# A layer step of a hybrid decoder on one NeuronCore: selected-value pages with two tokens in a row, and one copy of the turned probabilities

## The chip, the cores and the metric

The kernel runs on one core of one Trainium2 chip. The metric is device time in microseconds of one execution of the whole program; the profile is of one execution by the hardware profiler. Engines are called PE or TensorE (matrix products; PEld is its loading of weights), DVE or VectorE, ACT or ScalarE, POOL or GpSimd, and SP or SyncE, which here only issues transfers.

## The reference, cut to what matters

One decoder layer is computed for a prompt of 512 tokens and for 8 sample tokens, each with a cache of 2048 tokens in 16 pages of 128. The part that the change touches is the selected branch of the native sparse attention of the samples: the softmax over the selected blocks, times the cached values.

```python
kg, vg = ks[bi, idx], vs[bi, idx]
kpos = idx[..., None] * L_SEL + jnp.arange(L_SEL)
mask = kpos <= qpos[None, :, None, None]
sc = jnp.einsum('bqhd,bqjsd->bqhjs', q, kg) * ATTN_SCALE
...
o_sel = jnp.einsum('bqhjs,bqjsd->bqhd', p2.reshape(sc.shape).astype(q.dtype), vg)
```

There are 4 query heads, one shared head of keys and values, 64 channels, and everything is in fp32. The kernel does not gather blocks: it computes the probabilities for all 2048 cached tokens (zero where a block is not selected) and multiplies them with all 16 value pages of the sample.

## The kernel before, in words

**Order.** One list of steps, `TL`, made by `timeline()` (line 102), is walked by every engine; each engine does its part of a step and waits on semaphores. From `("out_z", 0)` on, the streams `head`, `units`, `join`, `cols` and `last` (lines 192 to 219) are merged by numbers that give each step a place. So PE's order is fixed, and on every engine a wait holds back all that follows.

**What runs between 250 and 370 us.** Three streams share PE. The MoBA units (`mu`, `mp`, lines 925 to 948; 32 units of four pages, of which 16 to 31 fall here) score and weigh one unit of four 256 KB pages each, out of a ring of four units, `moba_lo` and `moba_hi`. The columns of the prompt's attention (`cq`, `cv`, lines 740 to 798) are the largest part. The join of the samples (`stat` to `spv`) combines the branches.

**The join, for sample b.** `psc` (line 1751) multiplies `Psel`, the selected probabilities, by the branch weights. Psel holds four row groups of 32 partitions, j = 0 to 3, each with 4 heads and 512 tokens (8 pages of 64 tokens; j // 2 says which half of the page, j % 2 whether pages 0 to 7 or 8 to 15). `st` with c = 0 (line 982) turns it in four transposes of 128x128 into PSUM bank 2: partition = two pages' tokens of 64 each, column = row group and head. DVE then copies the four heads of each row group into `PTs` (lines 1763 to 1769). `st` with c = 1 does the same for the window branch (line 984; ACT copies it at 1250). `spv` (lines 986 to 1003) multiplies PTs with the values, 16 products with 128 tokens in the partitions, 4 columns of weights and 64 channels, adding into four places of PSUM bank 3 in turn.

**The value pages.** `selV`, one tile a sample, holds a page as 128 partitions (tokens) x 64 channels. The 128 pages are loaded by their numbers in `page_ids`: steps `("selv", n)` load four each, the even groups by SP (line 607) and the odd ones by POOL (line 1370). On SP they stand among the loads of the MoBA pages, `load_unit` (line 536), each of which waits until the unit four before it is done, and the weight panels (526).

Because psum's partition is (page parity, token of 64) for one half of the page, while a page in `selV` has all its 128 tokens in the partitions, the copy into PTs has to move halves of the partitions: two psum halves e (page parity) by two halves of the page, four copies of 64 partitions.

Of the kernel before, what the change touches and what calls it, by code (L numbers as in the profile page):

```python
# [5 lines left out]
F32 = mybir.dt.float32  # L6
# [8 lines left out]
P = 128  # L15
D = 1024
KT = D // P
T, B = 512, 8
NT = T + B
HALF = NT // 2  # L20
NX = NT + 2
H, HD = 4, 64
PAGE, PAGES = 128, 16
NPOOL = 160
# [272 lines left out]
def build(nc, a, o):  # L297
    ctx = ExitStack()
    with ctx:
# [5 lines left out]
        def place(name, shape, dt=F32, offset=None):  # L305
            size = 4
            for s in shape[1:]:
                size *= s
            if offset is None:
                offset = at[0]  # L310
                at[0] += (size + 31) // 32 * 32
            return nc.alloc_sbuf_tensor_at(name, shape, dt, offset=offset)
# [4 lines left out]
        o_op = at[0]  # L317
        opH = place("opH", [P, KT, NT], F32R)
        opL = place("opL", [P, KT, NT], F32R)
        o_raw = at[0]  # L320
# [14 lines left out]
        moba_hi = place("moba_hi", [P, 2, 4, 512], F32, o_a + 24576)  # L335
        moba_ring = [moba_lo[:, 0], moba_lo[:, 1], moba_hi[:, 0], moba_hi[:, 1]]

        selV = [place(f"selV{b}", [P, PAGES, HD], F32, o_raw + b * PAGES * HD * 4 if b < B - 1 else o_op + (KT + 6) * NT * 4) for b in range(B)]
        WB = place("WB", [B, 13, P], F32, o_op + 2 * NT * 4)

        hidH = [place(f"hidH{g}", [P, KT, NT], F32R, (o_z, o_op)[g]) for g in range(2)]
# [7 lines left out]
        std = place("std", [P, NT], F32, o_after_hid + 6 * NT * 4)  # L349
        lnt = place("lnt", [P, 4, NT], F32, o_after_hid + 7 * NT * 4)  # L350
        xsum, qsum, dmul, dmean = (lnt[:, q, :] for q in range(4))

        def centred(eng, n, k):

# [53 lines left out]
        Pc = place("Pc", [P, 2, P])  # L408
        PcT = place("PcT", [P, 2, P])
        PTm2 = place("PTm2", [P, 2, P], F32, o_z + 1024)  # L410
        PTs = place("PTs", [P, 2, 2, 8, H], F32, o_op + (KT + 2) * NT * 4 + 512)
        PTw = place("PTw", [P, 2, 4, H])
        st = place("st", [P, 256])
        ps_small = place("ps_small", [P, 32])
# [36 lines left out]
        psum = ctx.enter_context(nc.psum_tensor("psum", [P, 8, 512], F32))  # L451
# [64 lines left out]
        def _(sp_):  # L516
# [22 lines left out]
            for kind, n, *part in TL:  # L539
# [12 lines left out]
                elif kind == "load_w1":  # L552
                    sp_.dma_start(w1[:, :, :], a["w1"]).then_inc(w1_in, 16)
                    sp_.wait_ge(ids_in, 16)
                elif kind == "load_state":
                    sp_.dma_start(sc[:, :, :, :], a["state_convT"]).then_inc(state_in, 16)
                    sp_.dma_start(sp[:, :, :, :], a["state_poolT"]).then_inc(state_in, 16)
                elif kind == "load_nsa":
                    if n == 1:
                        sp_.wait_ge(cmp_mm, 1)  # L560
                    if n >= 2:
                        sp_.wait_ge(ssel_mm, n - 1)
                    for p, v in enumerate(pages(n * PAGES, PAGES)):
                        sp_.dma_start(nsa_ring[:, n % 2, p, :],
                                      a["nsa_pages"][bass.ds(v, 1)].rearrange("a p n -> (a p) n")).then_inc(nsa_in[n % 2], 16)
                elif kind == "load_post":
                    sp_.wait_ge(ssel_mm, B)
                    sp_.wait_ge(kc_done, B + 1)
                    sp_.dma_start(winK[:, :, :], a["winK"]).then_inc(win_in, 16)
                    sp_.dma_start(winV[:, :, :, :], a["winV"]).then_inc(win_in, 16)  # L570
                    load_unit(2)
                    load_unit(3)
                elif kind == "out_early":
                    read(sp_, ("mm", PANEL_SLOT.index(S_PO + 1)))
                    sp_.dma_start(o["z_cmp"], zT[:, S_CMP, :]).then_inc(out_early, 16)
                    sp_.dma_start(o["pool_prompt"], zT[:, S_PO:S_PO + 2, T - 15:T]).then_inc(out_early, 16)
                elif kind == "out_conv":
                    sp_.wait_ge(glu_done, 2)
                    sp_.dma_start(o["conv_prompt"], zc[:, :, T:T + CW - 1]).then_inc(out_conv, 16)
                    sp_.dma_start(o["conv_sample"], sc[:, :, :, :]).then_inc(out_conv, 16)  # L580
                    sp_.wait_ge(pool_d, 1)
                    sp_.dma_start(o["pool_sample"], sp[:, :, :, :]).then_inc(out_conv, 16)
                elif kind == "load_lo":
                    sp_.wait_ge(conv_done, 1)
                    sp_.wait_ge(cpw_mm, 2)
                    sp_.wait_ge(pool_mm, 2)
                    sp_.wait_ge(out_conv, 16 * 3)
                    load_unit(0)
                    load_unit(1)
                elif kind == "out_z":  # L590
                    read(sp_, ("mm", N_IN_PANELS - 1))
                    sp_.dma_start(o["z_ksel"], zT[0:HD, S_KSEL, :]).then_inc(out_z, 16)
                    sp_.dma_start(o["z_kwin"], zT[0:HD, S_KWIN, :]).then_inc(out_z, 16)
                    sp_.dma_start(o["z_v"], zT[:, S_V, :]).then_inc(out_z, 16)
                    sp_.dma_start(o["z_moba"], zT[:, S_MK:S_MK + 4, :]).then_inc(out_z, 16)
                elif kind == "zrow" and n == 0:
                    bank_read(sp_, 0, ("zrow", 0))
                    sp_.dma_start(o["win_sample"][:, T - 1, 0:HD], zs[:, 3, 0:HD]).then_inc(out_rows, 16)
                    sp_.dma_start(o["win_sample"][:, T - 1, HD:P], zs[:, 2, HD:P]).then_inc(out_rows, 16)
                elif kind == "mp" and n + 4 < MU:  # L600
                    sp_.wait_ge(mp_mm, n + 1)
                    load_unit(n + 4)
                elif kind == "selv" and n // 4 % 2 == 0:
                    if n == 0:
                        sp_.wait_ge(mm_done, N_IN_PANELS)
                    for p, v in enumerate(pages(4 * n, 4), 4 * n):
                        sp_.dma_start(selV[p // PAGES][:, p % PAGES, :],  # L607
                                      a["selv_pages"][bass.ds(v, 1)].rearrange("a p n -> (a p) n")).then_inc(selv_in[p // PAGES], 16)
                elif kind == "load_x" and n == 1:
                    sp_.wait_ge(st_mm, 2 * B)  # L610
                    sp_.dma_start(xres[:, :, :], a["xT"]).then_inc(x_in, 16)
                elif kind == "ln" and n == 0:

                    sp_.dma_start(o["win_sample"][:, 0:T - 1, :], a["state_win"][:, 1:T, :]).then_inc(out_state, 16)
                elif kind == "y":
                    for k in Y_ORDER:
                        sp_.wait_ge(ln_n, KT + Y_ORDER.index(k) + 1)
                        sp_.dma_start(o["y"][:, k, :], xres[:, k, :]).then_inc(out_y, 16)
# [9 lines left out]
        def _(pe):  # L628
            mm = nc.tensor.matmul
# [178 lines left out]
            for step in TL:  # L808
# [16 lines left out]
                elif kind == "zcols":  # L825
# [5 lines left out]
                    for t in range(QT):  # L831
                        last = nc.tensor.transpose(psum[:, 4, t * NGATE:(t + 1) * NGATE], zT[0:NGATE, S_GATE, t * P:(t + 1) * P], ident[0:NGATE, 0:NGATE])
                    last.then_inc(zc_mm, 1)
                    for t in range(QT):
                        last = nc.tensor.transpose(psum[:, 5, t * P:(t + 1) * P], zT[:, S_V, t * P:(t + 1) * P], ident)
                    last.then_inc(zc_mm, 1)
                elif kind == "zrow":
# [3 lines left out]
                    for j, slot in enumerate(ROW_SLOTS[n]):  # L841
                        m = NGATE if slot == S_GATE else P
                        last = nc.tensor.transpose(psum[0:B, n % 2, j * P:j * P + m], zT[0:m, slot, T:NT], ident[0:m, 0:m])
# [21 lines left out]
                elif kind == "pool":  # L865
                    acc_wait(step)
                    pe.wait_ge(pool_d, n + 1)
                    for hf in range(2):
                        last = mm(acc(step)[:, hf, 0:HALF], vec[:, V_PO + n * P:V_PO + (n + 1) * P], pb[:, hf * HALF:(hf + 1) * HALF],
                                  start=True, stop=True)  # L870
# [115 lines left out]
                elif kind == "spv":  # L986

                    b = n
# [5 lines left out]
                    V = selV[b]  # L994
                    for k in range(2):
                        bank_read(pe, 2, ("st", b, k))
                    for p in range(PAGES):
                        mm(out[p % 4], PTs[:, b % 2, p // 8, p % 8, :], V[:, p, :], start=False, stop=False, skip_group_check=True)
                    for w in range(4):
                        mm(out[w], PTw[:, b % 2, w, :], winV[:, b, w, :], start=False, stop=False, skip_group_check=True)  # L1000

# [311 lines left out]
        def _(pool):  # L1313
# [12 lines left out]
            for kind, n, *part in TL:  # L1326
# [35 lines left out]
                if kind == "selv" and n // 4 % 2 == 1:  # L1362
# [4 lines left out]
                    pool.wait_ge(mp_mm, MU1 + 2 * n // 5 - 2)  # L1367
                    for p in range(n * 4, n * 4 + 4):
                        v = pool.value_load(page_ids[0:1, p:p + 1])
                        pool.dma_start(selV[p // PAGES][:, p % PAGES, :],  # L1370
                                       a["selv_pages"][bass.ds(v, 1)].rearrange("a p n -> (a p) n")).then_inc(selv_in[p // PAGES], 16)
                elif kind == "xsum":

# [37 lines left out]
        def _(dve):  # L1411
# [22 lines left out]
            for step in TL:  # L1434
# [324 lines left out]
                elif kind == "st" and part[0] == 0:  # L1759
                    dve.wait_ge(st_mm, 2 * n + 1)  # L1760
                    if n >= 2:
                        dve.wait_ge(spv_mm, n - 1)
                    for e in range(2):
                        s = psum[HD * e:HD * e + HD, 2, :].rearrange("p (s j x) -> p s j x", s=4, j=4)
                        for half in range(2):
                            last = nc.vector.tensor_copy(
                                PTs[HD * half:HD * half + HD, n % 2, :, e:8:2, :].rearrange("p g s h -> p s g h"),
                                s[:, :, 2 * half:2 * half + 2, 0:H])
                    last.then_inc(bfree[2], 1)
                elif kind == "mpv":  # L1770
                    dve.wait_ge(mpv_mm, 1)
# [103 lines left out]
def layouts(x):  # L1875
# [81 lines left out]
    for n in range(2):  # L1957
# [5 lines left out]
        "panels": f(np.stack([p.reshape(P, D) for p in panels])),  # L1963
        "w_gate": f(panel(w_in, allr, r(c0[3], NGATE)).reshape(P, KT * NGATE)),
        "nsa_pages": f(np.concatenate([cmpT, selK], 2)),
        "selv_pages": f(nsa[:, :, 3]),
        "moba_pages": f(np.concatenate([mK, mV], 2)),
        "winK": f(winK), "winV": f(winV), "state_win": f(win.reshape(B, T, P)),
        "state_convT": rows(x["state_conv"][0]),
# [37 lines left out]
```

## Time and profile before

| | |
|---|---|
| time, three runs | 816.41 us median (815.53, 816.41, 818.66) |
| the profiled execution: its time | 813.84 us |
| its span, first to last instruction | 812.2 us |
| PE busy | 762.4 us (94%) |
| DVE, ACT, POOL busy | 455.4, 287.9, 180.6 us |
| moved by DMA | 113.20 MB, 66123 packets |
| of them under 512 B | 16985 packets |
| mean granted TensorE clock | 0.980 of 2.4 GHz |

"Busy" is the time in which an engine has at least one instruction in work; a matmul's end is modelled, so a busy PE is not PE at its peak. "Idle before" in a row of the timeline is how long the engine stood still ahead of the row, with the instruction that released it. A wait for several semaphores is put down to the one that came last. The DMA share is the mean busy share of the 16 DMA engines.

### The profile page before, as it was taken

To read this page: it belongs to the slowest core of one execution; us is meant where nothing else is said; L and a number is where in the kernel's file an instruction comes from. 1 tells how busy PE (TensorE), PEld (TensorE's weight loads), DVE (VectorE), ACT (ScalarE), POOL (GpSimd) and SP (SyncE) were. 2 spreads that over 40 slices of the span, in tenths; PEclk is the share of its full clock that TensorE was granted. 3 is DMA by queue.
4 is the path that set the end of the run, shared out by engine and by line. 5 is a ranking of instruction groups with operands and counts; after the bars stand their busy time and mean duration, and the time that the engine had idled before them with its cause. 6 is when DMAs were issued, how large, how long until landed. Compare 5 with 4: busy or idle time off the path is not lost.

```text
span 812.2 us, 17202 instructions
## 1 busy us (share of the span) xinstructions
PE 762.4 (94%) x6779; PEld 658.9 (81%) x6779; DVE 455.4 (56%) x832; ACT 287.9 (35%) x572; POOL 180.6 (22%) x212
## 2 busy tenths in 40 slices
PE   5999889889898899999999999999999999999992
PEld 5988768765454345449999999999999999999992
DVE  4269985356675655455876566533563336533435
ACT  4322225346456222333443444411432223321124
POOL 0000834000002535000555752100210011100083
PEclk9999999989999989999999999999999999999997
DMA  9546674464678879803243233432233223333202
GB/s 333 163 117 172 173 192 112 130 234 159 203 243 285 251 223 296 269 28 88 70 136 124 79 90 98 126 91 92 79 92 104 91 78 96 100 94 96 61 1 106
DMA packets 66123, 113.20 MB, mean 139 GB/s; under 512 B 16985, under 2 KB 34010, under 8 KB 65370
## 3 DMA queue, kind: packets, MB, share of 16 engines
q1 hardware_dynamic: 63994, 109.99, 43.9%
q0 software_dynamic: 2048, 2.10, 0.9%
q8 instruction: 54, 0.88, 0.5%
q14 instruction: 27, 0.22, 0.1%
HBM read 107.63 MB, written 6.52 MB: 141 GB/s over the span
## 4 chain that ended last, share of the span: by engine, by line
PE 69%; DVE 14%; SPq 6%; ACT 4%; issue 4%; DMA 1%; ACTq 0%; DVEq 0%
PE psum L680 55%; DVE yc L1504 4%; SPq L607 3%; SPq L536 2%; PE psum L733 2%; PE psum L689 2%; DVE wL L1442 1%; PE psum L946 1%; PE psum L764 1%; PE psum L935 1%; PE psum L796 1%; SPq L530 1%; DMA moba_lo<-in_moba_pages 1%; DVE nmR L1531 1%; PE psum L767 1%
## 5 line engine op out<-in xcount | busy, mean ns | idle before, releaser
L1442 DVE TENSOR_TENSOR wL<-raw,wH 128x1024 fp32r<-128x1024 f32 x90 | 117.1, 1301 | 114.8 <-ACT wH L1094 114.8
L1094 ACT ACTIVATE wH<-raw 128x1024 fp32r<-128x1024 f32 x90 | 93.7, 1042 | 123.8 <-PE psum L680 119.9
L680 PE MATMUL psum<-oxH,wH 128*128 128x260 f32 (+1 forms) x512 | 105.1, 286 | 1.5 <-DVE wL L1442 0.9
L680 PE MATMUL psum<-oxH,wL 128*128 128x260 f32 (+1 forms) x512 | 103.9, 284 | 0.0
L680 PE MATMUL psum<-oxL,wH 128*128 128x260 f32 (+1 forms) x512 | 103.4, 283 | 0.0
L680 PE MATMUL psum<-hidH,wL 128*128 128x260 f32 x512 | 103.2, 283 | 0.0
L680 PE MATMUL psum<-hidH,wH 128*128 128x260 f32 x512 | 103.2, 283 | 0.0
L680 PE MATMUL psum<-hidL,wH 128*128 128x260 f32 x512 | 103.0, 283 | 0.0
L680 PE MATMUL psum<-opH,wH 128*128 128x260 f32 (+1 forms) x416 | 88.4, 294 | 14.0 <-DVE opL L1438 8.4
L680 PE MATMUL psum<-opL,wH 128*128 128x260 f32 (+1 forms) x416 | 84.3, 285 | 0.0
L680 PE MATMUL psum<-opH,wL 128*128 128x260 f32 (+1 forms) x416 | 84.3, 284 | 0.0
L680 PEld LDWEIGHTS psum<-opH,wH 128*128 128x128 f32 (+1 forms) x416 | 64.1, 188 | 23.4 <-issue 11.2
L1406 POOL TENSOR_TENSOR hsq<-relu 128x520 f32<-128x520 f32 x32 | 33.7, 1054 | 218.7 <-ACT relu L1276 218.7
L680 PEld LDWEIGHTS psum<-oxH,wH 128*128 128x128 f32 x512 | 79.5, 189 | 3.3 <-issue 2.4
L680 PEld LDWEIGHTS psum<-oxL,wH 128*128 128x128 f32 x512 | 79.9, 190 | 0.0
L680 PEld LDWEIGHTS psum<-oxH,wL 128*128 128x128 f32 x512 | 79.4, 189 | 0.0
L680 PEld LDWEIGHTS psum<-hidH,wH 128*128 128x128 f32 x512 | 79.0, 189 | 0.1
L680 PEld LDWEIGHTS psum<-hidH,wL 128*128 128x128 f32 x512 | 78.9, 188 | 0.0
L680 PEld LDWEIGHTS psum<-hidL,wH 128*128 128x128 f32 x512 | 78.7, 188 | 0.0
L1822 DVE SCALAR_TENSOR_TENSOR xres<-xres,psum 128x520 f32<-128x520 f32 x32 | 22.2, 695 | 90.0 <-PE psum L680 90.0
L1370 POOL DMA_DIRECT2D selV<-in_selv_pages x64 | 34.5, 540 | 159.0 <-issue 141.5
L680 PEld LDWEIGHTS psum<-opL,wH 128*128 128x128 f32 (+1 forms) x416 | 63.9, 187 | 0.4
(348 smaller groups left out, 1154.0 us busy)
## 6 DMA issues: line engine op xcount, KB each, us to landing
raw<-in_panels SPq DMA_DIRECT2D x89, 512.0 KB, 3.6
moba_lo<-in_moba_pages SPq DMA_DIRECT2D x64, 256.0 KB, 4.0
moba_hi<-in_moba_pages SPq DMA_DIRECT2D x64, 256.0 KB, 4.0
nsa_ring<-in_nsa_pages SPq DMA_DIRECT2D x128, 96.0 KB, 2.2
xres<-in_xT SPq DMA_DIRECT2D x8, 260.0 KB, 6.6
xres<-in_xT SPq DMA_DIRECT2D x1, 2080.0 KB, 8.7
out_y<-xres SPq DMA_DIRECT2D x8, 260.0 KB, 2.1
selV<-in_selv_pages POOLq DMA_DIRECT2D x64, 32.0 KB, 3.7
```

The costliest lines, as they stand in the source:

```text
L530: return nc.values_load_multi_w_load_instructions(page_ids[0:1, first:first + n], [mybir.EngineType.SP])[1]
L536: sp_.dma_start(moba_ring[q % 4][:, p, :], a["moba_pages"][bass.ds(v, 1)].rearrange("a p n -> (a p) n")).then_inc(moba_in[q % 4], 16)
L607: sp_.dma_start(selV[p // PAGES][:, p % PAGES, :], a["selv_pages"][bass.ds(v, 1)].rearrange("a p n -> (a p) n")).then_inc(selv_in[p // PAG ...
L680: last = mm(out[0:M, hf, 0:cols], w, x[:, k, hf * HALF:hf * HALF + cols], start=(t == 0 and j == 0), stop=(t == KT - 1 and j == 2))
L689: last = mm(psum[:, 4, kv * 256:kv * 256 + n], w1[:, kv * 8 + r, :], rhs(kv, r), start=(r == 0), stop=(r == 7))
L733: mm(psum[:, b + e, 0:m], zT[base:base + HD, sq + t, i * P:(i + 1) * P], zT[base:base + HD, sk, 0:m], start=True, stop=False, skip_group_c ...
L1094: fn(wtiles(wH, wH3, n).rearrange("p a b -> p (a b)")[:, 0:m], raw[:, n % NRAW, 0:m], ACT.Copy).then_inc(h_done, 1)
L1370: pool.dma_start(selV[p // PAGES][:, p % PAGES, :], a["selv_pages"][bass.ds(v, 1)].rearrange("a p n -> (a p) n")).then_inc(selv_in[p // PA ...
L1406: nc.gpsimd.tensor_tensor(hsq[:, up_no % 2, :], relu[:, up_no % 2, :], relu[:, up_no % 2, :], ALU.mult).then_inc(sq_done, 1)
L1442: tt(wtiles(wL, wL3, n).rearrange("p a b -> p (a b)")[:, 0:m], raw[:, n % NRAW, 0:m], wtiles(wH, wH3, n).rearrange("p a b -> p (a b)")[:, ...
L1504: stt(yc[:, t, 0:T], zc[:, t, k:k + T], w, yc[:, t, 0:T], ALU.mult, ALU.add).then_inc(vtap, 1)
L1822: stt(x, x, ALPHA if g == 0 else 1.0, acc(("mm", n))[:, :, 0:HALF], ALU.mult, ALU.add).then_inc(acc_read[1], 1)
```

## The change

The host lays out each value page as 64 rows of 512 bytes: row r holds the channels of token r and, behind them, those of token 64 + r. `selV` keeps its size, 4 KB a partition, but is now [128, 8, 128]: page p goes to the 64 partitions of its parity, at place p // 2. A place then has, in its partitions, the same order as the turned probabilities (page parity, token of 64), and its column half is the half of the page. So PTs can have PSUM's own order (q, j, head) and is filled by one copy of 128 partitions. The 16 products of a sample choose the place and the column half. The numbers of loads, products and bytes stay.

```diff
-        selV = [place(f"selV{b}", [P, PAGES, HD], F32, o_raw + b * PAGES * HD * 4 if b < B - 1 else o_op + (KT + 6) * NT * 4) for b in range(B)]
+        selV = [place(f"selV{b}", [P, PAGES // 2, P], F32, o_raw + b * PAGES * HD * 4 if b < B - 1 else o_op + (KT + 6) * NT * 4) for b in range(B)]
...
+        def selv_page(p):
+
+            half = p % 2
+            return selV[p // PAGES][HD * half:HD * half + HD, p % PAGES // 2, :]
...
-        PTs = place("PTs", [P, 2, 2, 8, H], F32, o_op + (KT + 2) * NT * 4 + 512)
+        PTs = place("PTs", [P, 2, 4, 4, H], F32, o_op + (KT + 2) * NT * 4 + 512)
...
-                        sp_.dma_start(selV[p // PAGES][:, p % PAGES, :],
+                        sp_.dma_start(selv_page(p),
                                       a["selv_pages"][bass.ds(v, 1)].rearrange("a p n -> (a p) n")).then_inc(selv_in[p // PAGES], 16)
...
-                    for p in range(PAGES):
-                        mm(out[p % 4], PTs[:, b % 2, p // 8, p % 8, :], V[:, p, :], start=False, stop=False, skip_group_check=True)
+                    for q in range(4):
+                        for j in range(4):
+                            half, pg = j // 2, j % 2
+                            mm(out[j], PTs[:, b % 2, q, j, :], V[:, pg * 4 + q, HD * half:HD * half + HD],
+                               start=False, stop=False, skip_group_check=True)
...
-                        pool.dma_start(selV[p // PAGES][:, p % PAGES, :],
+                        pool.dma_start(selv_page(p),
                                        a["selv_pages"][bass.ds(v, 1)].rearrange("a p n -> (a p) n")).then_inc(selv_in[p // PAGES], 16)
...
-                    for e in range(2):
-                        s = psum[HD * e:HD * e + HD, 2, :].rearrange("p (s j x) -> p s j x", s=4, j=4)
-                        for half in range(2):
-                            last = nc.vector.tensor_copy(
-                                PTs[HD * half:HD * half + HD, n % 2, :, e:8:2, :].rearrange("p g s h -> p s g h"),
-                                s[:, :, 2 * half:2 * half + 2, 0:H])
+                    s = psum[:, 2, :].rearrange("p (s j x) -> p s j x", s=4, j=4)
+                    last = nc.vector.tensor_copy(PTs[:, n % 2, :, :, :], s[:, :, :, 0:H])
                     last.then_inc(bfree[2], 1)
...
-        "selv_pages": f(nsa[:, :, 3]),
+        "selv_pages": f(nsa[:, :, 3].reshape(NPOOL, 2, HD, HD).transpose(0, 2, 1, 3).reshape(NPOOL, HD, P)),
```

On VectorE the program around the first sample's copy reads, before the change (PTm is the turned MoBA probabilities, own and OM the outputs of a MoBA unit, st the row maxima):

```order
L1613 TENSOR_REDUCE st<-psum 128x1 [waits ms_mm]
L1614 TENSOR_REDUCE st<-psum 128x1
L1617 COPY PTm_117<-psum 128x128 [waits mt_mm]
L1766 COPY PTs<-psum 64x4x2x4 [waits st_mm]
L1766 COPY PTs<-psum 64x4x2x4 x3
L1623 TENSOR_TENSOR own<-psum,cst 128x256 [waits mp_mm]
L1626 TENSOR_REDUCE OM<-own 128x64 [waits bank_free1]
L1751 TENSOR_TENSOR Psel<-Psel,Wt 128x512 [waits om_done]
```

and with the change, at the same place:

```order
L1621 TENSOR_REDUCE st<-psum 128x1 [waits ms_mm]
L1622 TENSOR_REDUCE st<-psum 128x1
L1625 COPY PTm_117<-psum 128x128 [waits mt_mm]
L1772 COPY PTs<-psum 128x64 [waits st_mm]
L1631 TENSOR_TENSOR own<-psum,cst 128x256 [waits mp_mm]
L1634 TENSOR_REDUCE OM<-own 128x64 [waits bank_free1]
L1759 TENSOR_TENSOR Psel<-Psel,Wt 128x512 [waits om_done]
```

Nothing else moved: one row in place of four, with the same waits. PE's program has the same rows in the same order, and on SP and POOL only the shape of the load differs, 64x128 for 128x64.

## Rows read from the trace of the kernel before

**Rows 1.** The page: busy times, and busy tenths in 40 slices of 20.3 us
```profile
PE 762.4 (94%) x6779; PEld 658.9 (81%) x6779; DVE 455.4 (56%) x832; ACT 287.9 (35%) x572; POOL 180.6 (22%) x212
...
DMA  9546674464678879803243233432233223333202
```

**Rows 2.** By stretch: us, busy PE, PEld, DVE, ACT, POOL; clock, DMA share, GB/s
```profile
255.00:293.00 38.00, 33.63 (x294) 15.77 (x292) 23.82 (x84) 13.40 (x33) 15.48 (x29) 0.87 0.77 239
293.00:335.00 42.00, 41.63 (x617) 21.41 (x615) 23.12 (x75) 11.03 (x32) 17.10 (x32) 1.00 0.91 281
```

**Rows 3.** Waits of PE, 255 to 345 us: total, times, longest
```profile
PE psum L946 <- DVE PTm L1617: 4.4, 3, 2.7
PE psum L935 <- DMA moba_lo<-in_moba_pages: 0.8, 2, 0.4
```

**Rows 4.** PE in order of time: start us, us, instructions, [idle before]
```profile
276.47 0.64 PE L935 MATMUL psum<-moba_lo,QM 128*32 128x128 f32 x16 [0.41 <-DMA moba_lo<-in_moba_pages]
...
285.18 1.08 PE L946 MATMUL psum<-moba_lo,PTm 128*32 128x256 f32 x8 [2.69 <-DVE PTm L1617]
...
323.01 0.68 PE L935 MATMUL psum<-moba_lo,QM 128*32 128x128 f32 x16 [0.37 <-DMA moba_lo<-in_moba_pages]
...
344.70 0.64 PE L946 MATMUL psum<-moba_hi,PTm 128*32 128x256 f32 x8 [0.63 <-DVE PTm L1617]
```

**Rows 5.** Chain of waits that ended last: shares by line, 255 to 323.1; long pieces
```profile
by line: SPq L607 34.7%; SPq L536 25.4%; issue 18.7%; SPq L530 10.6%; DMA moba_lo<-in_moba_pages 9.7%; SPq L526 1.1%; PE psum L935 0.4%; SPq L521 0.0%
...
256.14 1.12 SPq L607
...
307.04 1.01 SPq L536
```

**Rows 6.** The tiles PTs and PTm: ns min/median/max, first and last start
```profile
L998 PE MATMUL psum<-selV,PTs x256: 219/219/220, 300.3 to 341.2; 128*4 128x64 f32 x128
L1766 DVE COPY PTs<-psum x32: 182/189/195, 293.9 to 335.1; 64x32 f32<-64x32 f32 x32
...
L1617 DVE COPY PTm<-psum x32: 269/279/292, 189.0 to 344.4; 128x128 f32<-128x128 f32 x32
```

**Rows 7.** DVE in order of time, in the same columns
```profile
293.86 0.80 DVE L1766 COPY PTs<-psum 64x32 f32<-64x32 f32 x4 [2.50 <-PE psum L982]
294.69 0.43 DVE L1623 TENSOR_TENSOR own<-psum,cst 128x256 f32<-128x256 f32 x1
...
334.55 0.80 DVE L1766 COPY PTs<-psum 64x32 f32<-64x32 f32 x4 [0.94 <-PE psum L982]
...
343.26 0.42 DVE L1623 TENSOR_TENSOR own<-psum,cst 128x256 f32<-128x256 f32 x1 [1.87 <-PE psum L946]
```

**Rows 8.** Waits of DVE, 293 to 345 us
```profile
DVE own L1623 <- PE psum L946: 13.8, 8, 2.2
DVE st L1613 <- PE psum L935: 6.3, 5, 1.9
DVE PTs L1766 <- PE psum L982: 4.9, 4, 2.5
```

**Rows 9.** Issues on SyncE: ns min/median/max, first and last start
```profile
L607 SPq DMA_DIRECT2D selV<-in_selv_pages x64: 332/333/1125, 255.6 to 327.3; - x64
...
L536 SPq DMA_DIRECT2D moba_hi<-in_moba_pages x64: 332/333/1119, 163.8 to 332.1; - x64
```

**Rows 10.** DMA queues, 303 to 304.6 us, then 129 to 134 us
```profile
q1 hardware_dynamic: 351, 0.08, 22.9%
...
q1 hardware_dynamic: 1396, 0.95, 76.6%
```

**Rows 11.** The page: GpSimd's DMA queue (packets, MB, share of 16 engines)
```profile
q0 software_dynamic: 2048, 2.10, 0.9%
```

**Rows 12.** By stretch, around a fall of the clock, columns as in rows 2
```profile
282.00:287.00 5.00, 2.31 (x22) 1.21 (x21) 3.59 (x23) 1.37 (x3) 2.85 (x6) 0.82 0.83 227
287.00:293.00 6.00, 6.00 (x36) 3.22 (x36) 3.09 (x9) 1.49 (x5) 0.03 (x1) 0.58 0.70 203
```

## The prediction

> **What bounds the kernel now.** I read the views from coarse to fine. First the page: PE is busy for 762.4 of 812.2 us, so TensorE is where time is lost or won, and everything that the change touches happens between 255 and 345 us, in the 13th to 17th of the 40 slices [rows 1]. There the DMA share is 7 to 9 tenths too, so a reader may suspect the DMA engines. The busy time by stretch separates the two: PE has 41.63 us of work in the 42 us from 293 to 335, while the DMA engines are 91% busy; from 255 to 293 PE has 33.63 of 38 us and the DMA share is 0.77 [rows 2]. So PE is full where the selected values are used, and the DMA engines are close behind it.
>
> Next, what PE waits for in the whole stretch: 4.4 us on VectorE's copy PTm (line 1617) and only 0.8 us, in two waits, on a DMA (a MoBA page) [rows 3]. The PE rows in order of time place them [rows 4]: 0.41 us before 276.47 and 0.37 us before 323.01 wait for MoBA pages; 2.69 us before 285.18 and 0.63 us before 344.70 wait for PTm. The third wait for PTm, 1.1 us by subtraction, is an earlier one, ahead of the first PTs copy.
>
> The chain of waits of this stretch tells another story at first sight: from 255 to 323 us it is SyncE's queue for 71.8% (34.7 in line 607, which issues the selected-value pages, 25.4 in 536, 10.6 in 530, 1.1 in 526), because one wait of PE of 0.37 us leads back into a queue that never rests [rows 5]. That chain has no more to give than the waits that it ends in: PE worked nearly all the time beside it. I read it as "SyncE has no slack", not as "SyncE costs 68 us".
>
> **The change, part by part.**
>
> *TensorE.* Each sample has the same 16 products of PTs (4 columns) with 64 columns of selV, in the same rotation over four output places, with the same two waits ahead of them. Shapes are equal, 219 ns for one [rows 6], so this part counts 0.
>
> *VectorE, one copy for four.* Now four copies of 64x32 take 0.80 us from first start to last end, eight times, 189 ns each alone [rows 6, 7]. The new copy has 128 partitions and 64 elements. It is not in the trace; the nearest rows bound it from both sides: 189 ns for 64x32, 279 ns for PTm's 128x128, also from PSUM [rows 6, 7]. I take 0.22 us, a third of the way, as 64 elements lie a third of the way from 32 to 128. VectorE saves 0.80 - 0.22 = 0.58 us a sample, 4.6 us in eight (4.2 to 4.9 by the bounds). How much of it reaches PE? From 293 to 345 VectorE itself waits for PE: 13.8 us ahead of "own", 6.3 ahead of the maximum, 4.9 ahead of these very copies [rows 8]. Behind the copies on its engine stand "own", the maximum and PTm, on which PE's MoBA products wait. Where a copy group delays them ("own" at 294.69 starts the moment the group ends [rows 7]), PE does not idle afterwards. The one PE wait on VectorE in the stretch, 0.63 us at 344.70, comes 9 us after the last group has ended (334.55 + 0.80), behind an "own" that waited 1.87 us for PE [rows 4, 7]. So 4.6 us are saved on VectorE, 0 on the path. The cover is PE's own work, 41.63 of 42 us, beside 23.12 of VectorE [rows 2]; were it gone, the groups could cost what they last, 4.6 us, which is a rival below.
>
> *Descriptors.* A page goes from 128 rows of 256 bytes to 64 of 512, the bytes stay. SyncE and GpSimd issue as many loads as before, 64 each, in the same place of their queues; an issue takes 333 ns on SyncE for selected-value rows and as much for MoBA rows of eight times the bytes [rows 9], so the issue count and its usual price stay. What a page costs the DMA engines: from 303 to 304.6 us only selected-value pages are on the queues. SyncE's 351 packets take 22.9% of 16 engines x 1.6 us = 5.9 us, 16.7 ns each; with 128 data packets and 16 that signal the end a page is 2.40 us, 0.150 us on 16 engines. From 129 to 134 us only the compressed-branch pages run, with 768-byte rows: 1396 packets in 76.6% of 80 us, 43.9 ns each, 6.32 us for a page of 144 packets and three times the bytes [rows 10]. A straight line through both gives 0.0612 us per KB and 3 ns per packet, so the new page, 80 packets and 32 KB, costs 1.96 + 0.24 = 2.20 us of engine time; the ends are 1.96 (no cost per packet at all) and 2.40 (no gain). The 64 pages of SyncE save 0.8 us on 16 engines, 1.8 us at best. GpSimd's pages already go as 2048 packets for 64 pages, a mean of 1 KB [rows 11], so I give them no gain; the bound is the same 1.8 us.
>
> What is it worth? At most what PE waits for DMA, 0.78 us, and at least nothing. The saving is spread over 80 us, and the wait before 323.01 ends 67 us into them, that before 276.47 after 21; a MoBA page lands earlier by what the pages just ahead of it in the full engines save, 0.0125 us each (0.0275 at best), and more where SyncE's queue has gained from it. With some ten pages ahead that is 0.1 to 0.3 us at each wait. I take half of the sum of both waits, **0.4 us**.
>
> The Trainium skill says otherwise of the rows now in use: "DMA: Bandwidth & Descriptors", section Specifications, wants at least 512 B for full rate, since a smaller one makes the engine read, modify and write. If a 256-byte row cost twice its bytes, the new page would cost half and both DMA waits would go: the sum would be 0.8 us in place of 0.4. The trace speaks against a factor of two: per byte the 256-byte page costs 3 x 2.40 / 6.32 = 1.14 times the 768-byte page [rows 10].
>
> *SyncE's long issues.* Seven of its issues between 255 and 323 us take 0.69 to 1.12 us in place of 0.33, 4.4 us too much together [rows 5]. If fewer descriptors shorten them, SyncE gains up to 4.4 us, but PE again no more than the 0.78 us already counted.
>
> **Sum:** 0 (PE) + 0 (VectorE) + 0.4 (DMA) = 0.4 us less. The profiled execution took 813.84 us (span 812.2), which makes 813.4; the median of the three runs is 816.41, so I predict **816.0 us**, no change that can be measured. A measurement of this kernel tells about 0.5%, 4.1 us, from no change.
>
> **The rivals.**
>
> *Nothing at all.* The packet's price is all bytes and a page still costs 2.40 us: 816.4. For it: 1.14 is near 1. A rule of the skill would lead there: "SBUF — State Buffer", section Door 1, says that partitions 0 to 63 reach only half of the 16 ports, 218 GB/s at most; by it a page of 32 KB takes 0.150 us. That is exactly what the page costs now in rows 10, so the gain on descriptors would be eaten by ports; no row here shows a load of half the partitions on its own. Chance 0.25; it is the same verdict.
>
> *VectorE was the pace-setter after all.* The 4.6 us pass through, 811.8 us, faster by 0.56%. For it: the groups of PTs copies stand between MoBA's steps on VectorE, and PE starts follow closely. Against: 0.6 us of PE waiting for VectorE in 52 us. 0.04.
>
> *SyncE's queue was it.* Its 4.4 us of long issues vanish and the chain shortens by them: 812.0 us. For it: 71.8% of the chain. Against: 0.8 us of PE waiting for DMA. 0.04.
>
> *Half the partitions slow every page (the other side).* Place: the 128 page loads, all ahead of or among MoBA's 1 MB units in the same engines. If a page's price doubles, SyncE's 64 pages add 9.6 us on 16 engines and GpSimd's 64 (0.9% of 812.2 us, 7.3 us for them all [rows 11]) another 7.3. The engines have 0.23 x 38 + 0.09 x 42 = 12.5 us free from 255 to 335 [rows 2]. It decides once a page is dearer by three quarters: MoBA pages then land late and PE stands still for at least 16.9 - 12.5 = 4.4 us. The clock adds to that: behind the PE gap of 2.69 us that ended at 285.18 the granted clock was at its lower level, 1.2 GHz, for a time (a mean of 0.82 and 0.58 in the two stretches) [rows 4, 12]. From 282 to 293 us 5 x 0.18 + 6 x 0.42 = 3.4 us are lost by it; I take half, 1.7 us, for one new, shorter gap. 816.4 + 4.4 + 1.7 = 822.5 us. Against: a long row has never been dearer than two short ones in these rows. 0.05.
>
> **How the numbers follow.** Forecast 0.62, nothing at all 0.25, the two fast rivals 0.08, the slow one 0.05. So faster by over 0.5%: 0.08; within 0.5%: 0.87; slower: 0.05. The range: the four execution times known of the kernel before are 813.84 to 818.66 us, without any change; moved by the forecast that is 813.4 to 818.3. The bounds of the unknown costs (0 to 0.78 us) lie inside. The rivals stay outside with 0.13 together.
>
> **What the new profile would show.** Right: eight PTs copies of 128 partitions near 0.22 us; VectorE's busy time down by 4 to 5 us, its waits for PE up by as much; SyncE's packets down by 4096; PE busy as before, its products of 219 ns unchanged; PE's waits for MoBA pages 0.4 us or less; the 2.69 us gap before 285 still there, as VectorE's softmax work stands before it. Wrong: a copy over 0.3 us; PE waits for selV or for moba_lo and moba_hi over 1 us, or a third stretch at the lower clock; or a span below 809 us with the groups of PE packed closer, which would mean that waits were hidden in what the profile counts as PE's busy time.

## The result, and the profile after

The changed kernel takes 824.94 us in the median of five runs (822.81 to 826.29), the kernel before 816.96 in five (815.53 to 818.66): ratio 1.0087, 95% interval 1.0059 to 1.0116. It is 8 us slower. I had forecast 816.0 within 813.4 to 818.3.

The page of the profiled execution (825.51 us, span 823.8), busy times and DMA share in 40 slices; the lines that answer to [rows 1]:

```profile
span 823.8 us, 17178 instructions
...
PE 767.0 (93%) x6779; PEld 661.0 (80%) x6779; DVE 450.5 (55%) x808; ACT 287.5 (35%) x572; POOL 179.4 (22%) x212
...
DMA  9446673454678777732134233332233322332202
...
DMA packets 62027, 113.20 MB, mean 137 GB/s; under 512 B 8793, under 2 KB 29914, under 8 KB 61274
```

VectorE has lost 4.9 us of work and the queues 4096 packets, as forecast. PE's work is up by 4.6 us, and no product was added; a part of the products ran at the lower clock. The engines that were to become cheaper did, and the kernel is slower. So the next view is what PE waits for, 250 to 370 us, against [rows 3]:

```profile
PE psum L940 <- DMA moba_hi<-in_moba_pages: 5.4, 4, 1.9
PE psum L940 <- DMA moba_lo<-in_moba_pages: 4.1, 2, 2.2
PE psum L951 <- DVE PTm L1625: 3.1, 3, 1.2
```

The waits for MoBA pages went from 0.8 to 9.5 us. They are six, each of 0.9 to 2.2 us; PE in order of time, against [rows 4] (the first, the second and the last of them):

```profile
280.74 0.85 PE L940 MATMUL psum<-moba_lo,QM 128*32 128x128 f32 x16 [2.16 <-DMA moba_lo<-in_moba_pages]
...
300.26 0.64 PE L940 MATMUL psum<-moba_hi,QM 128*32 128x128 f32 x16 [1.79 <-DMA moba_hi<-in_moba_pages]
...
346.12 0.64 PE L940 MATMUL psum<-moba_hi,QM 128*32 128x128 f32 x16 [1.93 <-DMA moba_hi<-in_moba_pages]
```

Yet the DMA engines are less busy than before; by stretch, in the columns of [rows 2]:

```profile
257.00:296.00 39.00, 34.14 (x296) 15.45 (x295) 23.85 (x84) 13.01 (x32) 14.97 (x29) 0.87 0.66 207
296.00:338.00 42.00, 36.53 (x508) 18.39 (x508) 16.47 (x45) 9.42 (x29) 16.52 (x32) 0.96 0.85 257
...
300.00:306.00 6.00, 5.74 (x43) 2.82 (x43) 2.45 (x7) 0.84 (x3) 3.56 (x7) 0.72 1.00 303
```

In the 42 us of the second stretch PE works 36.53 in place of 41.63, and the DMA share is 0.85 in place of 0.91. Over the whole stretch neither is full now, though the DMA engines still are for the six microseconds of the last row; so something in front of both must be short of time. The last row also shows the extra fall of the clock, 0.72 on average from 300 to 306, right behind the PE gap of 1.79 us before 300.26. In front of the DMA engines is the queue that issues. The issues of the selected-value pages, SyncE's and GpSimd's, and the new copy, all from the views of the tiles, against [rows 9] and [rows 6]:

```profile
L612 SPq DMA_DIRECT2D selV<-in_selv_pages x64: 468/468/1192, 257.9 to 338.8; - x64
...
L1378 POOL DMA_DIRECT2D selV<-in_selv_pages x64: 516/516/856, 254.4 to 331.6; - x64
...
L1772 DVE COPY PTs<-psum x8: 223/224/225, 296.6 to 344.3; 128x64 f32<-128x64 f32 x8
...
L1005 PE MATMUL psum<-selV,PTs x256: 218/219/221, 306.4 to 352.9; 128*4 128x64 f32 x128
```

One issue of a 64-row load holds SyncE for 468 ns; a 128-row load of the same page held it for 333. Sixty-four times 0.135 is 8.6 us (the 64 issues as they ran, with a few long ones among them, sum to 33.1 us against 25.2). The queue had none to spare: before the change SyncE's only wait from 255 to 340 us was one behind its last page, ahead of line 611:

```profile
SPq L611 <- PE psum L984: 5.0, 1, 5.0
```

In order of time, twelve pages ahead of a MoBA unit took 7.29 us before (first row) and take 8.73 now:

```profile
297.68 7.29 SPq L607 DMA_DIRECT2D selV<-in_selv_pages  x12
...
304.58 8.73 SPq L612 DMA_DIRECT2D selV<-in_selv_pages  x12
313.82 2.39 SPq L541 DMA_DIRECT2D moba_hi<-in_moba_pages  x4
```

In time: from PE's product on the sample rows (line 843 before, 848 now) to the first product of the output panels the stage lasts 368.89 - 252.56 = 116.3 us before and 380.62 - 254.93 = 125.7 after, 9.4 more. MoBA waits make 8.7 of that, one more stretch of 3.4 us at the lower clock 1.7, and the waits for PTm fell from 4.4 to 3.1, -1.3: together 9.1. The rest of the difference between the two profiled executions lies ahead of the stage, where the program is the same.

### The profile page after: what moved, and what is told of

Same layout as the page of the kernel before. It is cut to its first block, busy times and chain, and to the rows that moved or that the text cites. A ratio compares the mean times of both kernels' runs of the same rounds, so it can differ in the third digit from the quotient of the medians.

```text
span 823.8 us, 17178 instructions
## 1 busy us (share of the span) xinstructions
PE 767.0 (93%) x6779; PEld 661.0 (80%) x6779; DVE 450.5 (55%) x808; ACT 287.5 (35%) x572; POOL 179.4 (22%) x212
## 4 chain that ended last, share of the span: by engine, by line
PE 69%; DVE 14%; SPq 7%; ACT 4%; issue 4%; DMA 2%; ACTq 0%; DVEq 0%
PE psum L685 54%; DVE yc L1512 4%; SPq L612 3%; SPq L541 2%; PE psum L738 2%; PE psum L694 2%; DVE wL L1450 1%; PE psum L951 1%; PE psum L940 1%; PE psum L769 1%; PE psum L801 1%; DMA moba_hi<-in_moba_pages 1%; SPq L535 1%; PE psum L772 1%; DVE nmR L1539 1%
```

## The experiments

Three theories stood. **Issue**: SyncE's time per 64-row load, on a queue without slack. **Transfer**: rows of 512 bytes into half the partitions slow the DMA engines or the MoBA pages beside them (the slow rival of the prediction). **Copy**: the one copy does it. "Before" was run beside each and lies at 817.0 to 817.4 us.

### The copy and the loads apart

*e1_four_copies*: the new loads, the copy in four pieces.

```diff
-s = psum[:, 2, :].rearrange("p (s j x) -> p s j x", s=4, j=4)
-last = nc.vector.tensor_copy(PTs[:, n % 2, :, :, :], s[:, :, :, 0:H])
+for e in range(2):
+    s = psum[HD * e:HD * e + HD, 2, :].rearrange("p (s j x) -> p s j x", s=4, j=4)
+    for half in range(2):
+        last = nc.vector.tensor_copy(PTs[HD * e:HD * e + HD, n % 2, :, 2 * half:2 * half + 2, :], s[:, :, 2 * half:2 * half + 2, 0:H])
```

> The changed kernel with the new page loads, but PTs filled by four copies of 64x32 again (same values, same place). Issue theory (SyncE's issue of a 64-row load lasts 468 ns in place of 332, and its queue had no slack): the loads alone make the loss, so 824 to 826 us, ratio to before 1.008 to 1.011. Theory that the single copy of 128 partitions does the harm (it makes all wait for the latest): 817 us. If the copy brings a gain that the loads hide, 4.6 us of it at most: up to 829 us.

Measured: 824.96 us, ratio 1.009 (1.006 to 1.0121). With four copies the loss is the same, so the loads alone make all of it that can be seen.

*e2_one_copy*: the kernel before with its own loads and one copy. It leaves out the move of the halves, so the samples' selected branch is not computed rightly; the instructions otherwise stay.

```diff
-for e in range(2):
-    s = psum[HD * e:HD * e + HD, 2, :].rearrange("p (s j x) -> p s j x", s=4, j=4)
-    for half in range(2):
-        last = nc.vector.tensor_copy(PTs[HD * half:HD * half + HD, n % 2, :, e:8:2, :].rearrange("p g s h -> p s g h"), s[:, :, 2 * half:2 * half + 2, 0:H])
+s = psum[:, 2, :].rearrange("p (s j x) -> p s j x", s=4, j=4)
+last = nc.vector.tensor_copy(PTs[:, n % 2, :, :, :].rearrange("p g s h -> p (g s) h").rearrange("p (s j) h -> p s j h", s=4), s[:, :, :, 0:H])
```

> The kernel before with its own 128-row loads and one copy of 128x64 into PTs in place of four; the values of PTs then stand in wrong partitions, so the selected branch of the samples is wrong, all else is computed. Issue theory and the prediction's term for VectorE (0 on the path): 817 us, ratio 0.998 to 1.001, SyncE's issues of 332 ns, PE waits on DMA near 0.8 us. Theory that VectorE's 4.6 us reach the end: 812.4 us. Theory that the copy does the harm: 825 us.

Measured: 818.01 us, ratio 1.0009 (0.9984 to 1.0034). The copy is 224 ns here too, and neither brings nor costs anything that shows. The copy theory falls, and so does "VectorE was the pace-setter": 4.6 us less would be 0.9944, outside the interval.

### SyncE's time alone

*e3_sp_delay* and *e10_half_delay*: the kernel before, no transfer changed, but the page numbers of a group are fetched by three (two) register loads.

```diff
-for p, v in enumerate(pages(4 * n, 4), 4 * n):
+for p, v in enumerate([*pages(4 * n, 2), *pages(4 * n + 2, 1), *pages(4 * n + 3, 1)], 4 * n):   # e3
+for p, v in enumerate([*pages(4 * n, 2), *pages(4 * n + 2, 2)], 4 * n):                          # e10
```

> The kernel before with 128-row loads, but SyncE fetches the page numbers of each group of four selected-value pages with three register loads in place of one: 32 more of 0.30 us, 9.6 us more time of its queue, and no transfer changed. Issue theory: the same loss as the change, 824 to 828 us (ratio 1.007 to 1.013), with PE waiting 8 us or more for MoBA pages. Theory that rows of 512 bytes into half the partitions slow the transfers or the MoBA pages beside them: nothing of that is here, 817 us.

> The kernel before with one more register load of 0.30 us on SyncE for each group of four selected-value pages, 16 in all, 4.8 us (half the dose of the earlier delay, which cost 15 us for 9.6). Issue theory: SyncE's queue is the margin, so 3 to 8 us slower, 820 to 825 us; 817 us if a small delay is absorbed and only a large one shows.

Measured: 832.44 us (ratio 1.0166, 1.0123 to 1.0209) and 828.35 (1.014, 1.0117 to 1.0164). Both lose as the change does and more, without a 64-row load of selected values anywhere. PE's waits in e3, 250 to 380 us:

```profile
PE psum L935 <- DMA moba_lo<-in_moba_pages: 7.3, 2, 4.6
PE psum L935 <- DMA moba_hi<-in_moba_pages: 3.7, 2, 2.1
```

I had priced a register load at 0.30 us, 9.6 and 4.8 us in all, hence the misses of both expectations. The added loads took longer. All such loads on SyncE from 250 to 360 us, in the kernel before, in e3 and in e10:

```profile
L530 SPq TENSOR_LOAD <-page_ids x29: 294/300/601, 254.8 to 330.1; - x29
...
L530 SPq TENSOR_LOAD <-page_ids x63: 262/297/1732, 251.6 to 350.3; - x63
...
L530 SPq TENSOR_LOAD <-page_ids x46: 298/468/1716, 250.6 to 341.3; - x46
```

Those of the selected-value groups alone, summed one by one, are 16 loads of 5.1 us in all before, 48 of 18.9 in e3 and 32 of 16.6 in e10. So the doses were 13.8 us in e3 and 11.5 in e10, and the kernels lost 15.4 and 11.3: SyncE's added time is passed on nearly one to one. The sums are each of one execution, and the other issues of the queue vary by some us between executions (the 64 of selV sum to 25.2 us in before and 21.6 in e10), so no closer agreement is shown.

### The same transfers, with SyncE relieved

*e4_to_pool*: the changed kernel, sample 6 issued by GpSimd.

```diff
-elif kind == "selv" and n // 4 % 2 == 0:
+elif kind == "selv" and n // 4 % 2 == 0 and n // 4 != 6:
...
-if kind == "selv" and n // 4 % 2 == 1:
+if kind == "selv" and (n // 4 % 2 == 1 or n // 4 == 6):
```

> The changed kernel with the pages of sample 6 (16 of SyncE's 64) issued by GpSimd instead. All transfers, rows and copies are those of the change. Issue theory: SyncE saves 16 x 0.65 = 10.4 us and most of the loss goes: 816 to 819 us; GpSimd gets 80 pages and may become late for the last samples (PE waits for selV then), which would leave 820 to 822. Theory of slow transfers into half the partitions: the same transfers, so still 824 to 826 us.

Measured: 821.54 us, ratio 1.0055 (1.0034 to 1.0075). Only 3.4 of 8 us come back, where I had expected 5 or more, and it is not GpSimd's doing: PE never waited for selV. The relief came too late. Sample 6 stands at the end of the list, so SyncE gets spare time (7.7 us of waits for PE) only after 310, when the runs of pages ahead of the MoBA units are over. Its own row and the PE wait that stayed:

```profile
302.15 8.86 SPq L612 DMA_DIRECT2D selV<-in_selv_pages  x12
...
317.68 0.65 PE L940 MATMUL psum<-moba_hi,QM 128*32 128x128 f32 x16 [3.25 <-DMA moba_hi<-in_moba_pages]
```

So it may be that not only the sum counts but how many pages stand in a row ahead of a unit, and where. That led to the next pair.

*e8_alternate* and *e9_after_alternate*: SyncE takes the even groups of four pages and GpSimd the odd ones, in the kernel before and in the changed one. A semaphore of their own counts GpSimd's pages (the last sample shares the first one's).

```diff
-elif kind == "selv" and n // 4 % 2 == 0:
+elif kind == "selv" and n % 2 == 0:
...
-if kind == "selv" and n // 4 % 2 == 1:
+if kind == "selv" and n % 2 == 1:
...
-pe.wait_ge(selv_in[b], 16 * PAGES)
+pe.wait_ge(selv_in[b], 8 * PAGES)
+pe.wait_ge(selv_sw[b], 8 * PAGES * (1 + b // (B - 1)))
```

> The kernel before (128-row loads, four copies), but SyncE and GpSimd take the groups of four pages in turn in place of whole samples, so that SyncE never has 16 selected-value pages in a row between two MoBA units; counts and bytes as before. Issue theory: PE's waits for MoBA pages (0.8 us, in other executions up to 2.3) go to nothing: 815 to 817 us, ratio 0.997 to 1.000. If SyncE's total time is what counts, no change.

> The changed kernel with the same turn by turn issue. SyncE's total stays 8.7 us above that of before. If the total counts, 823 to 825 us; if the loss comes from runs of 12 and 16 pages ahead of a MoBA unit, 818 to 821 us.

Measured: e8 814.07 us, ratio 0.9966 (0.9952 to 0.998), faster than both kernels and than expected; PE's waits for MoBA pages are 0.6 us in its profiled execution, 0.8 in that of before, so the 3 us are not seen in these two profiles. e9 823.44 us, ratio 1.0083 (1.0055 to 1.0112): with 64 issues of 468 ns the order alone does not help, PE waits 9.2 us for MoBA pages. For e9 the sum decides, as one of the two expectations had it.

*e11_after_relieved* and *e12_relieved*: turn by turn, and every fourth of SyncE's groups to GpSimd, so 48 pages on SyncE and 80 on GpSimd; e11 with the new loads and one copy, e12 with the old loads and four.

```diff
-elif kind == "selv" and n % 2 == 0:
+elif kind == "selv" and n % 2 == 0 and n % 8 != 6:
...
-if kind == "selv" and n % 2 == 1:
+if kind == "selv" and (n % 2 == 1 or n % 8 == 6):
```

> The changed kernel (64 rows of 512 bytes, one copy) with the turn by turn issue and, besides, every fourth of SyncE's groups given to GpSimd: SyncE issues 48 pages, never more than 8 in a row, GpSimd 80. SyncE's time for pages is 48 x 0.65 = 31 us, below the 33 of before. Issue theory: all of the loss goes, 814 to 818 us, with PE waits on DMA under 2 us, although every transfer into half the partitions stays. Theory that something in these transfers or in the copy costs time of its own: 820 us or more.

> The same division of the issues (48 and 80 pages) on the kernel before, with 128-row loads and four copies. SyncE's time for pages is 48 x 0.52 = 25 us. Turn by turn alone gave 814.1 us with 0.6 us of PE waits on DMA left, so 813 to 815 us; if GpSimd with 80 pages comes late for a sample, PE waits for selV and it is 816 or more. Against the run beside it this is what the new layout costs or gives once SyncE has slack: 0 to 2 us by the issue theory.

Measured: e11 815.23 us, ratio 0.9969 (0.9952 to 0.9986), as the issue theory expected; e12 815.32, ratio 0.9973 (0.9951 to 0.9996), 0.3 above its expected range. Here the question is decided. e11 has every page in the change's form, with its issues still at 468 ns on SyncE, and loses nothing:

```profile
L1381 POOL DMA_DIRECT2D selV<-in_selv_pages x80: 516/516/866, 254.6 to 328.4; - x80
...
L614 SPq DMA_DIRECT2D selV<-in_selv_pages x48: 468/469/1382, 258.1 to 327.9; - x48
...
PE psum L953 <- DVE PTm L1628: 4.3, 3, 2.7
```

Among PE's waits from 250 to 380 us there is none for a DMA, in e11 or in e12. SyncE's waits for a MoBA unit to be done, its spare time, in e11 and in e12:

```profile
SPq L537 <- PE psum L953: 1.7, 2, 1.0
...
SPq L532 <- PE psum L948: 8.1, 4, 4.8
```

The 48 dearer issues, 48 x 0.135 = 6.5 us, come out of this spare time (8.1 - 1.7 = 6.4 us in these two executions) and not out of PE's. e11 and e12 stand within 0.1 us of each other: with spare time on SyncE the layout of 64 long rows and one copy is worth nothing that can be measured (each interval reaches some 1.5 to 2 us either way), neither 4.6 us of VectorE nor anything of the DMA engines. The transfer theory falls here: 48 of SyncE's 64 transfers and all of GpSimd's have the change's shape, so by it some three quarters of the loss, 6 us, should have stayed. From e9 to e11 only the issuing engine of 16 pages changes, and 8.2 us come back.

### What makes an issue dear

*e6_probe*: the kernel before, with eight extra loads on SyncE of each of eight shapes, in the feed-forward part (its time, 852.27 us, has these loads in it and is compared with nothing).

```diff
+for q, shape in enumerate(shapes):
+    for c in range(8):
+        to, fr = shape(bass.ds(pg[c % 4], 1), c)
+        sp_.dma_start(to, fr).then_inc(probe, 16)
+    sp_.wait_ge(probe, 16 * 8 * (q + 1))
```

> The kernel before, and in the feed-forward part, where SyncE has nothing to do, 64 extra loads on SyncE into a tile no longer used, eight of each of eight shapes with run-time page numbers: 128 rows of 256 B; 64 rows of 512 B into the lower and into the upper half of the partitions; 64 rows of 256 B; 128 rows of 512 B; 64 rows of 512 B out of a source with longer rows; 32 rows of 512 B; 128 rows of 128 B. If the number of rows sets the price of an issue, 332 ns for the shapes of 128 rows and 468 ns for all of 64 (another value for 32); if it is the row of 512 B, 468 ns for these at 128 rows too; if it is the merged or unmerged source, the sixth shape differs from the second; if the upper half, the third from the second.

The issues, shape by shape in the order of that text (ns min/median/max, start of the first and the last):

```profile
L632 SPq DMA_DIRECT2D Vn<-in_selv_pages x8: 333/351/815, 422.7 to 426.9; - x8
...
L632 SPq DMA_DIRECT2D Vn<-in_selv_pages x8: 526/546/573, 428.5 to 433.1; - x8
...
L632 SPq DMA_DIRECT2D Vn<-in_selv_pages x8: 469/546/547, 435.2 to 439.6; - x8
...
L632 SPq DMA_DIRECT2D Vn<-in_selv_pages x8: 468/546/547, 443.1 to 447.5; - x8
...
L632 SPq DMA_DIRECT2D Vn<-in_moba_pages x8: 332/362/381, 449.7 to 453.1; - x8
...
L632 SPq DMA_DIRECT2D Vn<-in_moba_pages x8: 480/546/547, 455.0 to 459.4; - x8
...
L632 SPq DMA_DIRECT2D Vn<-in_moba_pages x8: 338/370/372, 461.5 to 464.7; - x8
...
L632 SPq DMA_DIRECT2D Vn<-in_selv_pages x8: 352/381/383, 466.3 to 469.6; - x8
```

All four shapes with 64 rows take 468 to 573 ns, whether 256 or 512 bytes wide, lower or upper half, from a packed source or out of longer rows. The three shapes of 128 rows (256, 512 and 128 bytes) have medians of 351 to 381. In these shapes the width hardly matters; the number of rows does. And it is no rule of "fewer rows, dearer": 32 rows are 370.

*e7_short_rows*: the changed kernel, a page as 64 partitions x 2 runs of 256 bytes.

```diff
-return selV[p // PAGES][HD * half:HD * half + HD, p % PAGES // 2, :]
+return selV[p // PAGES][HD * half:HD * half + HD, p % PAGES // 2, :].rearrange("p (s n) -> p s n", s=2)
...
-a["selv_pages"][bass.ds(v, 1)].rearrange("a p n -> (a p) n")
+a["selv_pages"][bass.ds(v, 1)].rearrange("a (s p) n -> (a p) s n", s=2)
```

> The changed kernel, its pages again in the half of the partitions and read by one copy, but each page loaded as 64 partitions x 2 runs of 256 bytes (the host's layout is the one of before), so the row of 512 bytes is gone and the 64 partitions stay. Issue theory, by the probe (every load of 64 rows dear, whatever its width; 128 and 32 rows cheap): still 468 ns or more an issue and 824 to 829 us. If the count of descriptors sets the price of an issue (128 again), 332 ns and 817 us. Theory that the 512-byte rows did it: 817 us.

Measured: 833.87 us, ratio 1.0199 (1.0169 to 1.0228), slower than expected, for the issue got dearer still:

```profile
L612 SPq DMA_DIRECT2D selV<-in_selv_pages x64: 598/599/1617, 257.9 to 348.2; - x64
```

That is 0.266 us above 333 ns, 17.0 us for 64, and the kernel lost 16.8. The change itself paid 8.6 and lost 8.0. (GpSimd's issue is dearer too, 585 ns, but PE never waited for selV.) With e3 and e10 these are four doses on SyncE's queue, 8.6, 11.5, 13.8 and 17.0 us, and four losses, 8.0, 11.3, 15.4 and 16.8. Side by side:

| run | pages on SyncE, ns an issue | PE waits for MoBA pages, us | median, us |
|---|---|---|---|
| before | 64, 333 | 0.8 | 817.0 |
| after | 64, 468 | 9.5 | 824.9 |
| e1 new loads, four copies | 64, 469 | 7.6 | 825.0 |
| e2 old loads, one copy | 64, 333 | 2.3 | 818.0 |
| e7 64 x 2 x 256 B | 64, 599 | 15.3 | 833.9 |
| e10 old loads, 16 more register loads | 64, 333 | 7.8 | 828.4 |
| e3 old loads, 32 more register loads | 64, 333 | 11.0 | 832.4 |
| e4 sample 6 to GpSimd | 48, 468 | 6.4 | 821.5 |
| e9 new loads, in turn | 64, 469 | 9.2 | 823.4 |
| e11 new loads, relieved | 48, 469 | 0 | 815.2 |
| e12 old loads, relieved | 48, 333 | 0 | 815.3 |
| e8 old loads, in turn | 64, 333 | 0.6 | 814.1 |

## Why the prediction was wrong

*The step that failed* is in the part on descriptors: "an issue takes 333 ns on SyncE for selected-value rows and as much for MoBA rows of eight times the bytes [rows 9], so the issue count and its usual price stay." Both rows there are loads of 128 rows. They show that the width of a row does not matter there, and I took them to show that the shape does not. The change altered the one number that both rows shared. The term stood at nothing and was 0.135 us an issue, 8.6 us in 64. The new load was in no row of the trace, and I did not bound its price, as I had bounded the copy and the packet. Yet the trace of before had a warning that I did not read: SyncE's issues of other shapes. Two stores out of 64 partitions stand right ahead of the first selected-value load, at 0.53 and 0.59 us. A store is not a load, but they show that 333 ns is not every issue's price:

```profile
252.44 0.53 SPq L592 DMA_DIRECT2D out_z_ksel<-zT  x1
253.02 0.59 SPq L593 DMA_DIRECT2D out_z_kwin<-zT  x1
```

*The reading that should have caught it* was mine: "SyncE has no slack". The chain of waits went through SyncE for 71.8% [rows 5], and I concluded rightly that it had nothing to give, since PE waited only 0.78 us for a DMA. The other side of the same reading was left out. This queue never rested and just kept pace, so it passed nearly every microsecond added to it on to PE, while one taken from it could bring no more than what PE waited. The 0.78 us were a bound for the gain only; for a loss there was none. And even the bound for the gain was low: e8 gains 3 us in the median. The profiled execution of before (813.84 us) is faster than all its five timed ones; e2, with the loads and issues of before, had 2.3 us of waits for MoBA pages in its profile where before had 0.8. So that one profile may have undercounted what PE usually waits; no profile of a slower execution of before shows it.

*The rivals.* The one on the slow side had the direction, the place (MoBA pages late, PE gaps of some 2 us, an extra stretch at 1.2 GHz, as forecast for a new gap) and nearly the size, 822.5 us. Its mechanism was wrong: the transfers did not get dearer. SyncE's packets from 310 to 313 us, selected-value pages alone:

```profile
q1 hardware_dynamic: 354, 0.14, 17.3%
```

That is 8.3 us for 354 packets, 23.5 ns each, and 80 packets make 1.88 us a page, against 2.40 before [rows 10]; I had forecast 2.20, with 1.96 as the best end. The straight line had mixed two loads of the engines: packet by packet in these three windows, 256 bytes took 18 ns, 512 bytes 27 and 768 bytes 36 in the median (the 4-byte ones at the end 9), but the 768-byte ones averaged 48 in the fuller stretch that I had fitted. As I read the rule of the Trainium skill ("DMA: Bandwidth & Descriptors", Specifications), a page should have halved; the trace does not agree, it fell by 22%. By the Trainium skill ("SBUF — State Buffer", section Door 1) partitions 0 to 63 reach half of the ports, 218 GB/s at most. No run here tests that, and the agreement at 0.150 us that the prediction saw was a coincidence: in rows 10 it is engine time divided by 16, not the time that a page takes. The probe's loads into the lower half alone, 429.9 to 433.7 us:

```profile
q1 hardware_dynamic: 479, 0.20, 18.1%
```

They cost 23.0 ns a packet, 1.84 us a page, no more than in the change's alternation of halves; but 0.20 MB in 3.8 us is a mean of 52 GB/s, too little to show a limit of 218.

*The other rivals.* VectorE as the pace-setter is refuted by e2, and "nothing at all" by the loss. Of "SyncE's queue was it" the place was right and the side wrong: its long issues did not vanish, seven from 255 to 323 us still take 0.66 to 1.19 us (before it was eight, for one of 0.83 at 317.6 is missing from the prediction's seven).

*What held.* The copy: 0.224 us for 0.22 forecast, VectorE's busy time down by 4.9 for 4 to 5 and its waits for PE up, nothing of it on the path (e1 and after alike; e11 and e12 alike). The products on PE: 219 ns, unchanged. SyncE's packets: down by 4096. What did not hold beside the MoBA waits: the gap of 2.69 us ahead of PTm was to stay, and the longest is 1.2 now. That PE's waits on MoBA pages over 1 us would show the forecast wrong stood in the text, and they did. The 0.4 us of gain from the DMA engines is not seen: e11 and e12 differ by 0.1, with intervals of some 1.5 to 2 us either way.

*Still open:* why 64 rows are dear where 128 and 32 are not, why a register load on SyncE takes longer in e10 than in before, and where e8's 3 us come from.

## What to carry to other kernels

Before changing the shape of a load, look whether its issuing queue rests at all; if it never does, the price of one issue times their number is a term of the sum, and only rows of the same shape give it; where there is none, bound it by the dearest issue of that queue in the trace (here 0.53 and 0.59 us for 64 partitions). When a queue is just fast enough, as here, a saving on it is worth at most what others wait for it, while an addition is passed on nearly whole: bound the two sides separately. And where two engines share the issues, how they take turns can be worth more than what each transfer costs: here 3 us (0.34%) for a change of order, against nothing measurable for shorter transfers and fewer copies.

## What was not expected of the hardware

- SyncE's issue of a load, in the median: 64 rows 468 ns in the kernel (546 in the probe), 128 rows 333 (351 to 381), 32 rows 370 in the probe, and 64 partitions with two runs each 599. At 128 rows of 128, 256 and 512 bytes the probe's medians differ by 30 ns at most.
- GpSimd's issue of the same page went the other way, 534 to 516 ns in e12 and e11, with 128 and with 64 rows (585 with two runs in e7).
- A register load on SyncE, 300 ns in the median before, was 468 ns in e10 with one more per group.
